# V of the strided groups read back from a DRAM scratch, and rotary partners by a DVE shuffle

## The chip, the cores and the metric
The kernel runs on one core of one Trainium2 chip. The metric is device time in microseconds (us). Three runs of the kernel before gave 2353.53, 2354.49 and 2354.59 us; the median is 2354.49.

## The reference
The reference is a chain of one gated convolution block (three branches: pooling, short convolution, long convolution) and two attention layers with a convolutional feed-forward net, for 512 tokens of width 1024, all in float32. The change lies in the attention part of the two layers. Cut to it:

```python
proj = h @ w_in[l]                     # (512 x 1024) @ (1024 x 5120)
dq, dk, dv, sq, sk, sv, gate_logits = jnp.split(proj, splits, axis=-1)
dq = apply_partial_rope(dq.reshape(dshape), cos, sin)   # 3 groups, 4 heads of 64
dk = apply_partial_rope(dk.reshape(dshape), cos, sin)
# x1, x2 = first and second 8 of a head's first 16 channels:
# [x1 * cos - x2 * sin, x2 * cos + x1 * sin, rest]
y_a = dilated_attention(dq, dk, dv) @ w_proj_a[l]       # dilations 1, 4, 16
y_b = stick_breaking_attention(sq, sk, sv) @ w_proj_b[l]
```

In group g of the dilated attention a query attends to keys whose distance is a multiple of the dilation (1, 4 or 16). With 512 tokens, groups 1 and 2 attend only inside the four classes of tokens that are equal modulo 4.

## The kernel before
**Weights.** Every weight goes through one stream. SP loads chunks of 1 MB into two buffers `raw` (`chunk_load`, L559; it waits until the last piece of the chunk before the last has been split). A chunk has two pieces. ScalarE (ACT) copies a piece to float32r (`split_hi`, L448, executed at L456), VectorE (DVE) subtracts that from the original (`split_lo`, L458, executed at L463), and both parts lie in one of four buffers `whl`, three pieces ahead of use. TensorE (PE) multiplies each product in three passes: high with high, high with low, low with high (`passes`, L1582 to L1584).

**Tiles.** For most pieces `col_tile` holds the weights stationary and streams the activations `hT` (128 x 512): 24 matmuls a piece. For V (keys `sv` and `dv`) `token_tile` (L1762) does it the other way round: 128 tokens of `hT` are stationary and 256 columns of weights stream past, 48 matmuls a piece, so that V comes out with tokens on the partitions. For group 0 of `dv` the 128 tokens are neighbours; for groups 1 and 2 they are every fourth token, `slice(tb, SEQ, 4)`, so that each of the four token tiles is one class modulo 4. Tile after tile lies in two PSUM banks; ACT copies both at once into `vd` (L877).

**The loop that matters.** In each layer the list `DIL_KEYS` (L198) has 18 pieces, n = 0 to 17: six of `dq`, six of `dk`, six of `dv` (groups 0, 1, 2, two pieces each). PE, ACT and DVE each go through this list in the same order (L1824, L865, L1442), and each has hung on it the steps of the stick-breaking heads: head h has its scores behind piece 4h, its exponents behind piece 4h + 2, and its values behind piece 4h + 4. The exponents (L1807) wait for `splo`, which DVE writes in `sb_lo` (L1432, executed at L1434) in its step 4h + 1.

**Rotary partners.** ACT copies the 128 x 512 result of a `dq` or `dk` piece twice: rounded into `qhl` (L871) and in full into `qraw` (L872). DVE subtracts the two (`rope_lo`, L1400, executed at L1402). Two more PE passes multiply a permutation matrix `swap_r` with both parts (L1833, L1834) into bank 7; they stand behind the next piece. DVE then multiplies `qraw` with the cosines (L1410), bank 7 with the signed sines (L1413), and adds the two (L1420) into `qd` or `kd`, for groups 1 and 2 sorted by class.

**After the list.** PE goes on with eight units of two heads (L1884 holds their values): the scores of unit 0, then for each unit a piece of the gates, the transposes of the probabilities (L1867), the scores of the next unit, another piece of the gates, and the values (L1884), which read `vd`. On ACT stand, in this order, the last copy of V, the split of gate piece 3, and the exponentials of unit 0 (L897); on DVE the split of that piece, then the maxima (L1460, L1461). GpSimd (POOL) computes the roots of the norms (L613) and has nothing to do in the attention.

Of the kernel before, what the change touches and what calls it, by code (L numbers as in the profile page):

```python
# [31 lines left out]
P = 128  # L32
D = 1024
SEQ = 512
KT = D // P
TB = SEQ // P
LAYERS = 2
# [9 lines left out]
MASK = -1e30  # L47
TWO_PI = 2.0 * np.pi


# [4 lines left out]
for _name, _rows in VECS:  # L55
# [6 lines left out]

CONSTS = [("ident", 128), ("negtri", 128), ("swap", 128), ("sbmul", 128), ("corr", 64), ("freq", 1),
          ("sign", 1), ("sel", 256), ("mask", 512), ("sbadd", 128)]
# [8 lines left out]
def shape_constants():  # L73

    out = np.zeros((P, NCONST), np.float32)
    i = np.arange(P)

    def put(name, value):
        value = np.asarray(value, np.float32).reshape(P, -1)
        out[:, COFF[name]:COFF[name] + value.shape[1]] = value  # L80

    put("ident", np.eye(P))
    put("negtri", -(i[:, None] >= i[None, :]).astype(np.float32))
    swap = np.zeros((P, P))
    for p in range(P):
        if p % HEAD < ROPE_DIM:
            swap[p - p % ROPE_DIM + (p % ROPE_DIM + ROPE_DIM // 2) % ROPE_DIM, p] = 1.0
    put("swap", swap)
    put("sbmul", (i[:, None] < i[None, :]).astype(np.float32))
    put("sbadd", np.where(i[:, None] < i[None, :], 0.0, MASK))  # L90
    t = np.arange(16)
    put("corr", np.tile(np.concatenate([w / np.minimum(t + 1, w) for w in POOL_WINDOWS])[None], (P, 1)))
    inv = (np.float32(ROPE_THETA) ** (-np.arange(0, ROPE_DIM, 2, dtype=np.float32) / np.float32(ROPE_DIM)))
    put("freq", np.where(i % HEAD < ROPE_DIM, inv[i % (ROPE_DIM // 2)], 0.0))
    put("sign", np.where(i % ROPE_DIM < ROPE_DIM // 2, -1.0, 1.0))

    p = np.arange(256)
    put("sel", i[:, None] == 2 * (p // P) + p % P // HEAD)
    gap = i[:, None] - i[None, :]
    own = np.where(gap >= 0, 0.0, MASK)  # L100
    put("mask", np.concatenate([np.where(gap <= 0, 0.0, MASK), own, own,
                                np.where((gap >= 0) & (gap % 4 == 0), 0.0, MASK)], 1))
    return out
# [58 lines left out]
def build(nc, t, out):  # L162
# [82 lines left out]
    table = keep("table", [P, 2, SEQ])  # L245
    arena = at[0]

    negtri_r = nc.alloc_sbuf_tensor_at("negtri_r", [P, P], R, offset=tri_at)
    swap_r = nc.alloc_sbuf_tensor_at("swap_r", [P, P], R, offset=cst_at + 4 * COFF["negtri"])
    negones_r = nc.alloc_sbuf_tensor_at("negones_r", [P, P], R, offset=vcol_at)  # L250
# [47 lines left out]
    kd = over("kd", 12 * K, [P, 3, 2, SEQ])  # L298
    vd = over("vd", 24 * K, [P, 3, TB, 256])
    sbq = over("sbq", 36 * K, [P, 2, SEQ])  # L300
# [16 lines left out]
    rot = over("rot", 84 * K, [P, 2, SEQ])  # L317
    qhl = over("qhl", 48 * K, [P, 2, 2, SEQ], R)

    ff = over("ff", 0, [P, FT, 2, SEQ], R)  # L320
# [8 lines left out]
    negtri = cst[:, COFF["negtri"]:COFF["negtri"] + P]  # L329
    swapm = cst[:, COFF["swap"]:COFF["swap"] + P]  # L330
    sbmul = cst[:, COFF["sbmul"]:COFF["sbmul"] + P]
# [17 lines left out]
    with ctx:  # L349
# [5 lines left out]
        def sem(name):  # L355
# [20 lines left out]

        sp_hi, sp_lo, q_lo = sem("sp_hi"), sem("sp_lo"), sem("q_lo")
        rot_ps, rope_done, z_ps, sb_abs, sb_l, sp_ready, e_ps, sb_attn, sbo_ps, ob_hi, ob_lo = (
            sem(n) for n in ("rot_psum", "rope_done", "z_psum", "sb_abs", "sb_log", "sp_ready", "e_psum", "sb_attn",
                             "sbo_psum", "ob_hi", "ob_lo"))  # L380
# [5 lines left out]
        fconv, silu_done, ff_hi, ff_lo = (sem(n) for n in ("ffn_conv", "silu_done", "ff_hi", "ff_lo"))  # L386
        s_out, s_frow = sem("out_done"), sem("frow_in")
        dve_chain, act_chain, pool_chain = sem("dve_chain"), sem("act_chain"), sem("pool_chain")

# [209 lines left out]
        @block.gpsimd  # L599
        def _(pool):  # L600
            load_vectors(pool, [v for v in VECS if v[0] in SECOND_VECS], s_vec2)
            nc.gpsimd.memset(neghalf, -0.5).then_inc(pool_chain, 1)
            pool.wait_ge(pool_chain, 1)

            def first_lo(tb):

                pool.wait_ge(h_hi, 8 + tb + 1)
                nc.gpsimd.tensor_tensor(hT[:, 1, :, tb * P:(tb + 1) * P], cols8(xw(2, tb)), hT[:, 0, :, tb * P:(tb + 1) * P].bitcast(F),
                                        ALU.subtract).then_inc(h_lo, 1)

            for i_, (s, tb) in enumerate(ORDER):
                pool.wait_ge(s_ms, i_ + 1)
                nc.gpsimd.tensor_tensor(rstd[:, tb:tb + 1], msq[:, tb:tb + 1], neghalf[:, 0:1], ALU.pow).then_inc(s_rstd, 1)  # L613
                if (s, tb) == (1, 3):
                    first_lo(0)
                if s == 2 and tb >= 2:
                    first_lo(tb - 1)
                if (s, tb) == (2, 3):
                    first_lo(3)


        @block.scalar
        def _(act):
# [191 lines left out]
            for l in range(LAYERS):  # L815
# [49 lines left out]
                for n_, key in enumerate(DIL_KEYS(l)):  # L865
                    split_hi(W[key] + 3)
                    if key[0] in ("dq", "dk"):
                        w_wait_full(act, key)
                        if n_ >= 2:
                            act.wait_ge(rope_done, 12 * l + n_ - 1)  # L870
                        A(qhl[:, n_ % 2, 0, :], bank(W_BANK[key]), ACT.Copy, scale=HEAD ** -0.5 if key[0] == "dq" else 1.0)  # L871
                        A(qraw[:, n_ % 2, :], bank(W_BANK[key]), ACT.Copy,  # L872
                          scale=HEAD ** -0.5 if key[0] == "dq" else 1.0).then_inc(act_read, 1)
                    elif key[3] == 1:
                        w_wait_full(act, key)
                        b = W_BANK[key]
                        A(vd[:, key[2], :, :].rearrange("p a b -> p (a b)"), psum[:, b * SEQ:(b + 2) * SEQ], ACT.Copy).then_inc(act_read, 1)  # L877
                    h, ph = n_ // 4, n_ % 4
# [96 lines left out]
        def _(dve):  # L975
# [412 lines left out]
            for l in range(LAYERS):  # L1388
                s = 2 + 2 * l
                if l == 0:  # L1390
                    link(V.tensor_copy(negtri_r[:], negtri))
                    step(V.tensor_copy(swap_r[:], swapm))
                    step(V.tensor_copy(negones_r[:], negones[:]))
# [5 lines left out]

                def rope_lo(n_):  # L1400
                    await_read(dve, DIL_KEYS(l)[n_])
                    V.tensor_tensor(qhl[:, n_ % 2, 1, :], qraw[:, n_ % 2, :], qhl[:, n_ % 2, 0, :].bitcast(F), ALU.subtract).then_inc(q_lo, 1)  # L1402

                def rope(n_):
# [3 lines left out]
                    if n_:  # L1408
                        dve.wait_ge(rope_done, 12 * l + n_)
                    V.tensor_tensor(rot[:, 0, :], qraw[:, n_ % 2, :], table[:, 0, :], ALU.mult).then_inc(dve_chain, 1)  # L1410
                    chain[0] += 1
                    dve.wait_ge(rot_ps, 12 * l + n_ + 1)
                    link(V.tensor_tensor(rot[:, 1, :], bank(7), table[:, 1, :], ALU.mult))  # L1413
                    dst = (qd if isq else kd)[:, g, j, :]
# [27 lines left out]
                for n_, key in enumerate(DIL_KEYS(l)):  # L1442
                    split_lo(W[key] + 3)
                    if 1 <= n_ <= 12:
                        rope(n_ - 1)
                    if n_ < 12:
                        rope_lo(n_)
                    h, ph = n_ // 4, n_ % 4
# [119 lines left out]
        def _(pe):  # L1568
# [191 lines left out]
            for l in range(LAYERS):  # L1760
                s = 2 + 2 * l
                def token_tile(key, strided):  # L1762

# [7 lines left out]
                    for tb in range(TB):  # L1771
                        ts = slice(tb, SEQ, 4) if strided else slice(tb * P, (tb + 1) * P)
                        o_ = bank(b + tb // 2)[:, tb % 2 * 256:tb % 2 * 256 + 256]
# [9 lines left out]

                first_tiles([("sq", l, 0), ("sq", l, 1), ("sk", l, 0), ("sk", l, 1)], s)
                token_tile(("sv", l, 0), False)
                token_tile(("sv", l, 1), False)

# [36 lines left out]
                for n_, key in enumerate(DIL_KEYS(l)):  # L1824
                    if key[0] == "dv":
                        token_tile(key, key[2] > 0)
                    else:
                        col_tile(key, h_at(0), h_at(1))
                    if 1 <= n_ <= 12:

                        pe.wait_ge(q_lo, 12 * l + n_)
                        take(7)
                        M(bank(7), swap_r[:], qhl[:, (n_ - 1) % 2, 0, :], start=True, stop=False)  # L1833
                        M(bank(7), swap_r[:], qhl[:, (n_ - 1) % 2, 1, :], start=False, stop=True).then_inc(rot_ps, 1)  # L1834
                        give(7, rope_done, 12 * l + n_)
                    h, ph = n_ // 4, n_ % 4
# [35 lines left out]
                def dil_values(u):  # L1872
                    j, b = u // 4, u % 4
                    if u == 0:
                        await_read(pe, ("dv", l, 2, 1))
                    if b == 0:
# [3 lines left out]
                    for c in range(first_, 4):  # L1880
                        for e in range(2):
                            hs = slice((2 * j + e) * HEAD, (2 * j + e + 1) * HEAD)
                            v = vd[:, 0, b - 1 + c, hs] if c < 2 else vd[:, c - 1, b, hs]
                            ins = M(bank(6 + c // 2)[e * HEAD:(e + 1) * HEAD, b * P:(b + 1) * P], v, probT[:, e, c * P:(c + 1) * P],  # L1884
# [93 lines left out]
```

## Time and profile before

| what | value |
|---|---|
| median of three runs | 2354.49 us |
| the profiled execution | 2355.59 us, span 2353.7 us |
| PE busy | 2274.0 us, 97% |
| DVE, ACT, POOL busy | 53%, 34%, 1% |
| mean granted PE clock | 0.986 |
| chain that ended last | PE 92%, DVE 5% |
| DMA | 213.8 MB, 91 GB/s over the span |

The profiled execution took 1.1 us more than the median, and its span leaves 1.9 us of it outside. "Pitch" below is the distance between the starts of two neighbouring matmuls: since they overlap in the pipeline, the duration shown for one is longer than what it adds to the time. The clock is given as a share of 2.4 GHz: 1.00 is that level and 0.50 is 1.2 GHz.

### The profile page before, as it was taken

To read this page: it belongs to the slowest core of one execution; us is meant where nothing else is said; L and a number is where in the kernel's file an instruction comes from. 1 tells how busy PE (TensorE), PEld (TensorE's weight loads), DVE (VectorE), ACT (ScalarE), POOL (GpSimd) and SP (SyncE) were. 2 spreads that over 40 slices of the span, in tenths; PEclk is the share of its full clock that TensorE was granted. 3 is DMA by queue.
4 is the path that set the end of the run, shared out by engine and by line. 5 is a ranking of instruction groups with operands and counts; after the bars stand their busy time and mean duration, and the time that the engine had idled before them with its cause. 6 is when DMAs were issued, how large, how long until landed. Compare 5 with 4: busy or idle time off the path is not lost.

```text
span 2353.7 us, 25941 instructions
## 1 busy us (share of the span) xinstructions
PE 2274.0 (97%) x10818; PEld 1875.6 (80%) x10818; DVE 1249.8 (53%) x1633; ACT 790.5 (34%) x1136; POOL 33.1 (1%) x42
## 2 busy tenths in 40 slices
PE   3999999999999799999999999999999999999998
PEld 2788888887788688987688887888798768888887
DVE  7798797923545746222745554234622274555422
ACT  1223232322532344244343333134523434333311
POOL 1000000000000300000000000000000000000000
PEclk7999999999999899999999999999999999999999
DMA  9332233332233122122123323222211212323231
GB/s 295 115 107 93 94 99 97 103 100 90 72 106 114 54 90 69 40 72 72 56 70 108 107 92 105 88 75 89 72 54 55 73 63 80 108 92 101 94 99 72
DMA packets 185554, 213.80 MB, mean 91 GB/s; under 512 B 3680, under 2 KB 165086, under 8 KB 185438
## 3 DMA queue, kind: packets, MB, share of 16 engines
q1 hardware_dynamic: 184128, 210.52, 27.3%
q8 instruction: 86, 1.41, 0.3%
q10 hardware_dynamic: 1150, 1.57, 0.2%
q14 instruction: 30, 0.25, 0.0%
q0 software_dynamic: 160, 0.06, 0.0%
HBM read 210.03 MB, written 2.10 MB: 90 GB/s over the span
## 4 chain that ended last, share of the span: by engine, by line
PE 92%; DVE 5%; issue 1%; ACT 1%; POOL 0%; DMA 0%; SPq 0%; POOLq 0%; DVEq 0%; ACTq 0%
PE psum L1582 29%; PE psum L1584 28%; PE psum L1583 28%; PE psum L1807 1%; DVE adsum L1030 1%; PE psum L1796 1%; DVE whl L463 1%; PE psum L1819 1%; PE psum L1856 1%; PE psum L1884 1%; PE psum L1867 1%; DMA x<-in_x 0%; PE psum L1912 0%; DVE stat L999 0%; POOL stat L613 0%
## 5 line engine op out<-in xcount | busy, mean ns | idle before, releaser
L1582 PE MATMUL psum<-hT,whl 128*128 128x512 f32 (+1 forms) x2112 | 803.8, 381 | 9.2 <-DVE hT L1052 6.5
L1583 PE MATMUL psum<-hT,whl 128*128 128x512 f32 (+1 forms) x2112 | 796.3, 377 | 0.0
L1584 PE MATMUL psum<-hT,whl 128*128 128x512 f32 (+1 forms) x2112 | 795.9, 377 | 0.0
L463 DVE TENSOR_TENSOR whl<-raw,whl 128x1024 fp32r<-128x1024 f32 (+1 forms) x368 | 449.4, 1223 | 642.8 <-ACT whl L456 642.8
L456 ACT ACTIVATE whl<-raw 128x1024 fp32r<-128x1024 f32 (+1 forms) x368 | 384.7, 1048 | 484.1 <-PE psum L1584 446.4
L1582 PEld LDWEIGHTS psum<-hT,whl 128*128 128x128 f32 x2112 | 398.4, 189 | 91.4 <-DVE hT L1052 9.8
L1584 PEld LDWEIGHTS psum<-hT,whl 128*128 128x128 f32 x2112 | 398.4, 189 | 73.6
L1583 PEld LDWEIGHTS psum<-hT,whl 128*128 128x128 f32 x2112 | 398.6, 189 | 71.2 <-issue 0.7
L1582 PE MATMUL psum<-whl,hT 128*128 128x256 f32 (+1 forms) x384 | 139.9, 364 | 10.0 <-DVE gates L1532 6.2
L1582 PE MATMUL psum<-whl,ff 128*128 128x512 f32 x352 | 139.9, 397 | 2.2 <-DVE fsil L1561 2.2
L1583 PE MATMUL psum<-whl,ff 128*128 128x512 f32 x352 | 139.5, 396 | 0.0
L1584 PE MATMUL psum<-whl,ff 128*128 128x512 f32 x352 | 139.5, 396 | 0.0
L1583 PE MATMUL psum<-whl,hT 128*128 128x256 f32 (+1 forms) x384 | 138.1, 360 | 0.0
L1584 PE MATMUL psum<-whl,hT 128*128 128x256 f32 (+1 forms) x384 | 137.9, 359 | 0.0
L1582 PEld LDWEIGHTS psum<-whl,hT 128*128 128x128 f32 x384 | 91.5, 238 | 17.7 <-DVE gates L1532 7.0
L1584 PEld LDWEIGHTS psum<-whl,hT 128*128 128x128 f32 x384 | 91.6, 238 | 5.4
L1583 PEld LDWEIGHTS psum<-whl,hT 128*128 128x128 f32 x384 | 91.7, 239 | 5.0
L1093 DVE SCALAR_TENSOR_TENSOR hc<-glu,vcol,hc 128x512 f32<-128x512 f32 x120 | 89.3, 744 | 0.0
L1093 DVE SCALAR_TENSOR_TENSOR acc<-glu,vcol,acc 128x512 f32<-128x512 f32 x112 | 83.3, 744 | 0.1
L1552 DVE TENSOR_SCALAR facc<-apad,vcol 128x512 f32<-128x512 f32 x44 | 24.0, 547 | 110.9 <-ACT fsil L962 53.0
L1582 PEld LDWEIGHTS psum<-whl,ff 128*128 128x128 f32 x352 | 66.3, 188 | 18.9 <-issue 3.0
L1584 PEld LDWEIGHTS psum<-whl,ff 128*128 128x128 f32 x352 | 66.3, 188 | 16.2
(269 smaller groups left out, 2198.2 us busy)
## 6 DMA issues: line engine op xcount, KB each, us to landing
raw<-in_w_in SPq DMA_DIRECT2D x88, 1024.0 KB, 5.1
raw<-in_w_up SPq DMA_DIRECT2D x44, 1024.0 KB, 5.1
raw<-in_w_down SPq DMA_DIRECT2D x20, 1024.0 KB, 5.0
ada<-in_w_ada SPq DMA_DIRECT2D x12, 1024.0 KB, 11.0
raw<-in_w_branch SPq DMA_DIRECT2D x12, 1024.0 KB, 5.1
raw<-in_w_out SPq DMA_DIRECT2D x12, 1024.0 KB, 5.0
x<-in_x SPq DMA_DIRECT2D x4, 512.0 KB, 7.4
raw<-in_w_proj_b SPq DMA_DIRECT2D x2, 1024.0 KB, 4.9
```

Of the source, the lines that this page charges most:

```text
L456: nc.scalar.activation(whl_view(w, 0), raw_view(w), ACT.Copy).then_inc(w_hi, 1)
L463: nc.vector.tensor_tensor(whl_view(w, 1), raw_view(w), whl_view(w, 0).bitcast(F), ALU.subtract).then_inc(w_lo, 1)
L1030: ins = V.scalar_tensor_tensor(o_, at_k(k), cact[:, k:k + 1], o_, ALU.mult, ALU.add)
L1093: last[dst is acc1] = step(V.scalar_tensor_tensor(A_(dst), g[:, k:k + SEQ], col("cf_w", 8 * k + tt), A_(dst), ALU.mult, ALU.add))
L1552: link(V.tensor_scalar(facc[:], apad[:, j, 2:2 + SEQ], cw(2), col("conv_b", FT * l + f), ALU.mult, ALU.add))
L1582: M(out_, stat_hi, mov_hi, start=start, stop=False, **kw)
L1583: M(out_, stat_hi, mov_lo, start=False, stop=False, **kw)
L1584: return M(out_, stat_lo, mov_hi, start=False, stop=stop, **kw)
L1796: M(bank(2 + kb)[:, 0:SEQ - kb * P], sbk[rows, h // 2, kb * P:(kb + 1) * P], sbq[rows, h // 2, kb * P:], start=True, stop=True, skip_group ...
L1807: M(bank(2 + kb)[:, (jb - kb) * P:SEQ - kb * P], (negtri_r if jb == kb else negones_r)[:], part[:, SBO[jb]:SBO[jb + 1]], start=False, stop ...
L1819: ins = M(bank(6)[po:po + HEAD, kb * P:], sbv[:, kb, h * HEAD:(h + 1) * HEAD], sba[:, SBO[kb]:SBO[kb + 1]], start=kb == 0, stop=kb == TB - ...
L1856: ins = M(bank(2 + e)[:, a:z], qd[heads, g, j, b * P:(b + 1) * P], kd[heads, g, j, k0:k0 + z - a], start=False, stop=g == 2, skip_group_ch ...
```

## The change
The pieces of `dv` for groups 1 and 2 are computed from neighbouring tokens, like group 0. ACT copies them to `vnat`, waits for its own copy, and writes them with a DMA from its queue to a DRAM scratch `v_by_token`. POOL waits for that DMA and reads the scratch back into `vc`, four neighbouring rows to a partition, so that partition u holds tokens 4u to 4u + 3 and class r is a contiguous slice. The first values of PE wait for both reads. The permutation matrix, its two matmuls, `qhl`, the second copy of ACT and `rope_lo` are gone; DVE makes the partners with a shuffle of `qraw` inside blocks of 32 partitions. The matrix leaves the constants, and the working memory behind them begins at a multiple of 128 bytes.

```diff
-    arena = at[0]
+    arena = (at[0] + 127) // 128 * 128
...
-    vd = over("vd", 24 * K, [P, 3, TB, 256])
+    vd = over("vd", 24 * K, [P, TB, 256])
+    vc = over("vc", 28 * K, [P, 2, TB, 256])
+    vnat = over("vnat", 80 * K, [P, 2, TB, 256])
+    v_dram = nc.dram_tensor("v_by_token", (LAYERS, 2, SEQ, 256), F)
...
+                if s in (2, 4) and tb == 3:
+                    l = s // 2 - 1
+                    for g in range(2):
+                        pool.wait_ge(v_out[g], 16 * (l + 1))
+                        pool.dma_start(vc[:, g, :, :], v_dram[l, g].rearrange("(u r) n -> u r n", r=TB)).then_inc(v_class, 16)
...
-                        A(qhl[:, n_ % 2, 0, :], bank(W_BANK[key]), ACT.Copy, scale=HEAD ** -0.5 if key[0] == "dq" else 1.0)
...
-                        A(vd[:, key[2], :, :].rearrange("p a b -> p (a b)"), psum[:, b * SEQ:(b + 2) * SEQ], ACT.Copy).then_inc(act_read, 1)
+                        g = key[2]
+                        if g == 1:
+                            act.wait_ge(rope_done, 12 * l + 12)
+                        dst = vnat[:, g - 1, :, :] if g else vd[:]
+                        A(dst.rearrange("p a b -> p (a b)"), psum[:, b * SEQ:(b + 2) * SEQ], ACT.Copy).then_inc(act_read, 1)
+                        if g:
+                            await_read(act, key)
+                            act.dma_start(v_dram[l, g - 1].rearrange("(b p) n -> p b n", p=P), vnat[:, g - 1, :, :]).then_inc(v_out[g - 1], 16)
...
-                    V.tensor_tensor(rot[:, 0, :], qraw[:, n_ % 2, :], table[:, 0, :], ALU.mult).then_inc(dve_chain, 1)
-                    chain[0] += 1
-                    dve.wait_ge(rot_ps, 12 * l + n_ + 1)
-                    link(V.tensor_tensor(rot[:, 1, :], bank(7), table[:, 1, :], ALU.mult))
+                    swapped = step(V.stream_shuffle(rot[:, 1, :], qraw[:, n_ % 2, :], ROPE_SWAP))
+                    step(V.tensor_tensor(rot[:, 0, :], qraw[:, n_ % 2, :], table[:, 0, :], ALU.mult))
+                    dve.wait_ge(dve_chain, swapped)
+                    link(V.tensor_tensor(rot[:, 1, :], rot[:, 1, :], table[:, 1, :], ALU.mult))
...
-                    if n_ < 12:
-                        rope_lo(n_)
...
-                        ts = slice(tb, SEQ, 4) if strided else slice(tb * P, (tb + 1) * P)
+                        ts = slice(tb * P, (tb + 1) * P)
...
-                    if 1 <= n_ <= 12:
-
-                        pe.wait_ge(q_lo, 12 * l + n_)
-                        take(7)
-                        M(bank(7), swap_r[:], qhl[:, (n_ - 1) % 2, 0, :], start=True, stop=False)
-                        M(bank(7), swap_r[:], qhl[:, (n_ - 1) % 2, 1, :], start=False, stop=True).then_inc(rot_ps, 1)
-                        give(7, rope_done, 12 * l + n_)
...
-                        await_read(pe, ("dv", l, 2, 1))
+                        await_read(pe, ("dv", l, 0, 1))
+                        pe.wait_ge(v_class, 32 * (l + 1))
...
-                            v = vd[:, 0, b - 1 + c, hs] if c < 2 else vd[:, c - 1, b, hs]
+                            v = vd[:, b - 1 + c, hs] if c < 2 else vc[:, c - 2, b, hs]
```

## Rows read from the trace of the kernel before

**Rows 1.** The page: busy times, and the chain that ended last by engine.
```profile
PE 2274.0 (97%) x10818; PEld 1875.6 (80%) x10818; DVE 1249.8 (53%) x1633; ACT 790.5 (34%) x1136; POOL 33.1 (1%) x42
...
PE 92%; DVE 5%; issue 1%; ACT 1%; POOL 0%; DMA 0%; SPq 0%; POOLq 0%; DVEq 0%; ACTq 0%
```
**Rows 2.** Windows: length, PE, PEld, DVE, ACT, POOL busy, clock, DMA, GB/s.
```profile
879.10:910.70 31.60, 31.60 (x145) 24.81 (x145) 20.42 (x31) 16.01 (x30) 0.00 (x0) 1.00 0.21 67
943.70:1003.00 59.30, 58.14 (x277) 55.54 (x278) 11.68 (x16) 15.35 (x26) 0.00 (x0) 0.97 0.11 36
```
**Rows 3.** PE's weight loads: V of neighbouring, then of strided tokens.
```profile
945.90:951.90 6.00, 5.81 (x48) 1.00 0.00 0
...
967.40:989.90 22.50, 22.42 (x97) 1.00 0.15 47
```
**Rows 4.** PE in order of time: end of n = 13, all n = 14.
```profile
951.67 0.28 PE L1584 MATMUL psum<-whl,hT 128*128 128x256 f32 x1
953.11 0.48 PE L1582 MATMUL psum<-whl,hT 128*128 128x256 f32 x1 [1.16 <-ACT vd L877]
...
964.40 0.40 PE L1807 MATMUL psum<-sphi,negtri_r 128*128 128x512 f32 x1
```
**Rows 5.** PE: the permutation's two matmuls behind n = 1.
```profile
855.29 0.40 PE L1833 MATMUL psum<-qhl,swap_r 128*128 128x512 f32 x1
855.52 0.40 PE L1834 MATMUL psum<-qhl,swap_r 128*128 128x512 f32 x1
855.76 0.40 PE L1582 MATMUL psum<-hT,whl 128*128 128x512 f32 x1
```
**Rows 6.** DVE in order of time, step n = 5 of layer 0 (head 1).
```profile
889.16 1.12 DVE L1420 TENSOR_TENSOR qd<-rot 128x512 f32<-128x512 f32 x1
890.11 0.69 DVE L1402 TENSOR_TENSOR qhl<-qraw,qhl 128x512 fp32r<-128x512 f32 x1
890.71 1.48 DVE L1434 TENSOR_TENSOR splo<-sbs,sphi 128x1280 fp32r<-128x1280 f32 x1
```
**Rows 7.** Loads of L1807 in head 1; a DVE operation with one input.
```profile
L1807 PEld LDWEIGHTS psum<-sphi,negtri_r x4: 188/202/203, 893.1 to 896.0; 128*128 128x128 f32 x4
...
L1552 DVE TENSOR_SCALAR facc<-apad,vcol 128x512 f32<-128x512 f32 x44 | 24.0, 547 | 110.9 <-ACT fsil L962 53.0
```
**Rows 8.** ACT, then PE: list's end to first values, layer 0.
```profile
1003.92 1.02 ACT L877 ACTIVATE vd<-psum 128x1024 f32<-128x1024 f32 x1 [9.88 <-PE psum L1584]
...
1009.94 0.21 ACT L897 ACTIVATION_READ_ACCUMULATOR prob<-psum,stat 128x1 f32 x1
...
1010.59 0.81 PE L1867 MATMUL psum<-cst,prob 128*128 128x128 f32 x6
...
1018.53 0.88 PE L1884 MATMUL psum<-probT,vd 128*64 128x128 f32 x12
```
**Rows 9.** DMA issues: size, median us to landing; one issue on ACT.
```profile
x<-in_x SPq DMA_DIRECT2D x4, 512.0 KB, 7.4
...
raw<-in_w_down SPq DMA_DIRECT2D x4, 512.0 KB, 3.7
out<-x SPq DMA_DIRECT2D x4, 512.0 KB, 2.6
...
7.97 0.36 ACTq L636 DMA_DIRECT2D table<-in_b_ada  x1
```
**Rows 10.** POOL: its dearest DMA issue, and its first work after attention.
```profile
1.26 0.72 POOL L532 DMA_DIRECT2D vstage<-in_norm_mix  x1 [0.82 <-POOLq L1970]
...
1190.90 0.55 POOL L613 TENSOR_TENSOR stat<-stat 128x1 f32<-128x1 f32 x1 [372.88 <-DVE stat L1281]
```
**Rows 11.** What SP's queue waited for, in the whole span.
```profile
SPq L563 <- DVE whl L463: 2195.1, 186, 31.2
```
**Rows 12.** Windows within n = 14: PE busy, clock, DMA.
```profile
955.00:957.00 2.00, 2.00 (x11) 0.50 0.00 0
957.00:959.00 2.00, 2.00 (x10) 0.71 0.42 108
```

More of the change, by code:

```diff
@@ L48 @@
 TWO_PI = 2.0 * np.pi
+ROPE_SWAP = [(i + ROPE_DIM // 2) % ROPE_DIM if i < ROPE_DIM else i for i in range(32)]
 VECS = [("b_in", 96), ("pool_scale", 8), ("sc_w", 24), ("sc_b", 8), ("cf_b", 8), ("cf_ln_g", 8),
@@ L60 @@
 AV, AG, BB, BC, BH, BG, CA, CB, CG, MG = (8 * i for i in range(10))
-CONSTS = [("ident", 128), ("negtri", 128), ("swap", 128), ("sbmul", 128), ("corr", 64), ("freq", 1),
+CONSTS = [("ident", 128), ("negtri", 128), ("sbmul", 128), ("corr", 64), ("freq", 1),
           ("sign", 1), ("sel", 256), ("mask", 512), ("sbadd", 128)]
@@ L83, in shape_constants @@
     put("negtri", -(i[:, None] >= i[None, :]).astype(np.float32))
[L84 to L88, printed above, removed]
     put("sbmul", (i[:, None] < i[None, :]).astype(np.float32))
@@ L245, in build @@
     table = keep("table", [P, 2, SEQ])
-    arena = at[0]
+    arena = (at[0] + 127) // 128 * 128
     negtri_r = nc.alloc_sbuf_tensor_at("negtri_r", [P, P], R, offset=tri_at)
-    swap_r = nc.alloc_sbuf_tensor_at("swap_r", [P, P], R, offset=cst_at + 4 * COFF["negtri"])
     negones_r = nc.alloc_sbuf_tensor_at("negones_r", [P, P], R, offset=vcol_at)
@@ L317, in build @@
     rot = over("rot", 84 * K, [P, 2, SEQ])
-    qhl = over("qhl", 48 * K, [P, 2, 2, SEQ], R)
     ff = over("ff", 0, [P, FT, 2, SEQ], R)
@@ L329, in build @@
     negtri = cst[:, COFF["negtri"]:COFF["negtri"] + P]
-    swapm = cst[:, COFF["swap"]:COFF["swap"] + P]
     sbmul = cst[:, COFF["sbmul"]:COFF["sbmul"] + P]
@@ L375, in build @@
         row_full, row_read, s_ln, s_rt, s_pos, s_tab = (sem(n) for n in ("row_full", "row_read", "lnrow_in", "rot_steps", "pos_in", "tables_ready"))
-        sp_hi, sp_lo, q_lo = sem("sp_hi"), sem("sp_lo"), sem("q_lo")
-        rot_ps, rope_done, z_ps, sb_abs, sb_l, sp_ready, e_ps, sb_attn, sbo_ps, ob_hi, ob_lo = (
-            sem(n) for n in ("rot_psum", "rope_done", "z_psum", "sb_abs", "sb_log", "sp_ready", "e_psum", "sb_attn",
+        sp_hi, sp_lo = sem("sp_hi"), sem("sp_lo")
+        rope_done, z_ps, sb_abs, sb_l, sp_ready, e_ps, sb_attn, sbo_ps, ob_hi, ob_lo = (
+            sem(n) for n in ("rope_done", "z_psum", "sb_abs", "sb_log", "sp_ready", "e_psum", "sb_attn",
                              "sbo_psum", "ob_hi", "ob_lo"))
@@ L387, in build @@
         s_out, s_frow = sem("out_done"), sem("frow_in")
+        v_out, v_class = [sem("v_by_token_out0"), sem("v_by_token_out1")], sem("v_by_class_in")
         dve_chain, act_chain, pool_chain = sem("dve_chain"), sem("act_chain"), sem("pool_chain")
@@ L1391, in _ @@
                     link(V.tensor_copy(negtri_r[:], negtri))
-                    step(V.tensor_copy(swap_r[:], swapm))
                     step(V.tensor_copy(negones_r[:], negones[:]))
@@ L1398, in _ @@
                     split_lo(W[key] + 3)
-                def rope_lo(n_):
-                    await_read(dve, DIL_KEYS(l)[n_])
-                    V.tensor_tensor(qhl[:, n_ % 2, 1, :], qraw[:, n_ % 2, :], qhl[:, n_ % 2, 0, :].bitcast(F), ALU.subtract).then_inc(q_lo, 1)
                 def rope(n_):
@@ L1761, in _, with token_tile @@
                 s = 2 + 2 * l
-                def token_tile(key, strided):
+                def token_tile(key):
                     w = W[key]
@@ L1784, in _ @@
                 first_tiles([("sq", l, 0), ("sq", l, 1), ("sk", l, 0), ("sk", l, 1)], s)
-                token_tile(("sv", l, 0), False)
-                token_tile(("sv", l, 1), False)
+                token_tile(("sv", l, 0))
+                token_tile(("sv", l, 1))
                 def sb_scores(h):
@@ L1825, in _ @@
                     if key[0] == "dv":
-                        token_tile(key, key[2] > 0)
+                        token_tile(key)
                     else:
                         col_tile(key, h_at(0), h_at(1))
-                    if 1 <= n_ <= 12:
-                        pe.wait_ge(q_lo, 12 * l + n_)
-                        take(7)
-                        M(bank(7), swap_r[:], qhl[:, (n_ - 1) % 2, 0, :], start=True, stop=False)
-                        M(bank(7), swap_r[:], qhl[:, (n_ - 1) % 2, 1, :], start=False, stop=True).then_inc(rot_ps, 1)
-                        give(7, rope_done, 12 * l + n_)
                     h, ph = n_ // 4, n_ % 4
```

## The prediction
> **What bounds the kernel.** I read the page first: PE is busy 97% of the span and holds 92% of the chain that ended last [rows 1]. What PE does not execute is saved, and what the other engines do costs nothing until PE waits for it. Then the windows over the list of 18 pieces [rows 2]: a head's four steps take 31.6 us, all of them PE, with DVE at 20.4 and ACT at 16.0. The stretch of the V pieces takes 59.3 us; there DVE and ACT are nearly idle, and PEld, the weight loads, is busy nearly as long as PE. So I looked at the loads alone. With neighbouring tokens 48 loads take 5.81 us, 0.121 us each; with every fourth token 97 take 22.42, 0.231 each [rows 3]. Matmul shape, banks and engine are the same; the step of the stationary operand is what differs. In order of time the strided piece n = 14 lasts from 953.11 to 964.40, 11.3 us [rows 4]. One more thing is in the windows: at 955 to 959 the granted clock was at 0.50 and then 0.71 [rows 12], that is, at the 1.2 GHz level for some 3.4 us, shortly after PE had waited 1.16 us [rows 4], and the strided matmuls kept their pace (11 and 10 in 2 us). They were held by their loads and not by the array.
>
> **The change part by part.**
>
> *V from neighbouring tokens.* Four pieces a layer lose the stride, eight in all. A strided piece costs 48 x 0.231 = 11.1 us by the loads [rows 3] and 11.3 us by the start times [rows 4]; I take 11.25. A piece of neighbours costs 48 x 0.121 = 5.8. That is 8 x 5.45 = **43.6 us off**, all on PE's path. ACT and DVE have to follow at 5.8 us a piece, but they do so in the heads' steps, where a quarter of 31.6 us is 7.9 us for more work than stands here (11.7 us of DVE in 59.3 [rows 2]). SP's queue waits for DVE's splits 186 times [rows 11]: weights come early, at 67 GB/s in a head and 36 here. The wait of 1.16 us for the copy of group 0's V out of banks 0 and 1 [rows 4] stays, for the banks stay.
> The Trainium skill (SBUF — State Buffer, section Door 1: The DMA port swizzle) says that SBUF has lines of 16 bytes and wants two hits in each, yet also that one may stride for free as far as "4 fp32", which is the old step. By its first half the trace agrees, 0.231 against 0.121; by its second the stride was free and nothing of the 43.6 us would come. The rows decide for the first.
>
> *The permutation matmuls.* 24 pairs, each 0.47 us from 855.29 to 855.76 [rows 5]: **11.3 us off**. The first copy of ACT, the subtraction on DVE (0.69, in effect 0.60 from 890.11 to 890.71 [rows 6]) and DVE's wait for PE go too, for nothing by themselves: both engines have room in a head [rows 2]. Weight and matrix constants at the start: 64 KB less to load, nothing.
>
> *The shuffle.* It takes the place of the subtraction in DVE's queue, and behind it, in each head's second step, stands `splo`, for which PE's exponents wait. In head 1 `splo` ends at 890.71 + 1.48 = 892.19 and PE loads for it at 893.1 [rows 6, 7]: 0.9 us of slack. PE now comes two pairs earlier, 0.93 us, so the slack is gone, and what the shuffle takes beyond 0.60 PE waits for. This counts for heads 1 and 2 of both layers, four times; head 0 has a cheaper, unstrided add, and head 3 has no rope before its `splo`. No row shows a shuffle. From below 0.547 (one input, 128 x 512 [rows 7]), from above 1.12 (the strided add [rows 6]): 0 to 0.5 us each, 0 to 2 us in all. I take it like the subtraction it replaces, 0.69, for it reads and writes the same 128 x 512: **0.4 us added**.
> The Trainium skill (VectorE: DVE Perf Modes, section The perf-mode tier table) gives a shuffle about 2400 ns for 2048 elements a partition, by estimate 0.6 us for 512, which would make this 0.0 to 0.2 us; no row here shows it.
>
> *The writes.* ACT waits for the end of its copy (which otherwise overlaps the next by 0.1 us), then issues a DMA, 0.36 us for 512 KB at the start [rows 9]. For group 1 nothing urgent is behind it. For group 2 there is: ACT's split of gate piece 3, DVE's split and maxima, ACT's exponentials, PE's transposes. That chain ends at 1009.94 + 0.21 = 1010.15, and the transposes run from 1010.59, their load some 0.2 earlier [rows 8]: 0.2 us of slack against some 0.55 of delay. **0.7 us added** over two layers (0 if the issue is hidden, 1.5 if it takes the 0.72 of POOL's dearest issue [rows 10]).
>
> *The round trip.* The first values stand 14.6 us behind the start of the last V copy (1003.92 to 1018.53 [rows 8]). In that time: the copy and its wait 1.1; the write; POOL's issue 0.72 [rows 10]; the read. For 512 KB the rows have 2.6 (a store to DRAM), 3.7 (a load alone) and 7.4 (four loads at once at the start) [rows 9]. The write at 3.7, since a weight chunk may run beside it, and the read at 3.7: 1.1 + 3.7 + 0.7 + 3.7 = 9.2 us, covered with 5 us to spare. At 7.4 twice it is 16.6, 2.0 us late a layer, 4.0 in all. So **0, at most 4 us**. The cover is two gate pieces, a score unit and the transposes; without it all 9.2 us would show in each layer. Group 1's trip begins two pieces earlier. POOL's queue: its wait stands behind the norm of the layer and before its next root at 1190.90 [rows 10], some 180 us later. The other way about, 4 MB more beside 213.8: weights may land a few us later, while SP had been waiting for DVE, not for data [rows 11].
>
> *The clock.* The slow stretch was free because the strided loads held the pace. With neighbours nothing shows that holds them but the clock, so I take their 0.121 as doubled at 1.2 GHz: 3.4 us hold 14 matmuls instead of 28, **1.7 us lost**, in layer 0 if the stretch comes again; each further one would cost the same. None may come: 0 to 5 us.
>
> **The sum.** 43.6 + 11.3 = 54.9 off; 0.4 + 0.7 + 1.7 = 2.8 back; 52.1 net. The profiled execution took 2355.6 us: 2303.5. It stood 1.1 above the median, so beside 2354.5 I forecast **2302 us**. The bound above which a measurement of this kernel can be told from no change is 0.2%, 4.7 us.
>
> **Rivals.**
> 1. *The cover fails and the small waits add up.* The round trip shows by 4 us, the shuffle is dear (2 us, 1.6 more than taken), the clock falls twice more (3.4): 2302 + 9 = 2311 us. For it: the slack before `splo` is nil by my own working, and no row shows a DRAM write followed by a read. Against it: 5 us to spare in the trip. Chance 0.12.
> 2. *The stride was not what held the pace* (or the new loads are held as before): only the permutation's 11.3 us go, less 1.1 for the waits: 2354.5 - 10.2 = 2344 us. It is also what the page's "4 fp32" would give. Against it: everything but the stride is alike in [rows 3], and the pace did not follow the clock [rows 12]. Chance 0.03.
> 3. *Slower: PE stands at the first values until V is back.* The mechanism is one chain, ACT, DRAM, POOL, DRAM, with POOL's queue as the place where it could hang. A layer gains 26 us, so the point from which it decides is a read that lands 14.6 + 26 = 41 us behind the last copy, where I expect 9. At 50 us the stall is 35.4 a layer, 71 in all: 2354.5 - 52 + 71 = 2373 us. Against it: no transfer of 512 KB took over 7.4 us [rows 9]. Chance 0.02.
>
> **How the numbers follow.** The forecast has 0.83; its own range is 2298 (none of the 2.8 us, less 1 or 2 for scatter) to 2306. The range to give reaches to rival 1, 2298 to 2311, and leaves out some 0.1. Faster by over 0.2%: the forecast and rivals 1 and 2, 0.97. Within 0.2%: 0.01, a trip of just about 41 us. Slower: 0.02.
>
> **What the profile after would show.** The stretch of V without its strides: 48 loads of `hT` in 5.8 us for every piece, the stretch down from 59.3 to about 37 us. Four steps of a head at 29.7 instead of 31.6. No L1833. PE idle before the exponents under 0.2 us in heads 1 and 2. PE idle before the first values: none; reads landed some 9 us behind the start of the last copy. The transposes of unit 0 some 0.3 us late. I am wrong if the loads stay at 0.23, if a wait of several us stands before L1884, or if DVE's shuffle takes over 1.1 us.

## The result and the profile after

The changed kernel takes **2295.49 us** (median of 4 runs, 2294.41 to 2298.57) against 2354.54 for the kernel before, run beside it (4 runs, 2353.53 to 2356.69): the ratio is 0.975, interval 0.9733 to 0.9767. The forecast was 2302 us with a range of 2298 to 2311. The direction and nearly all of the size are right, and the time lies 2.5 us below the range. The profiled execution took 2294.44 us, span 2292.6, 61.1 less than before.

The page of the kernel after: busy times.
```profile
PE 2214.4 (97%) x10758; PEld 1822.4 (79%) x10770; DVE 1250.4 (55%) x1656; ACT 779.0 (34%) x1112; POOL 35.4 (2%) x46
```
Beside [rows 1]: 48 weight loads fewer, the 24 pairs of the permutation; PE 59.6 us less busy and still at 97%. It also holds 91% of the chain that ended last. The bound is the same engine, so nearly the whole saving is time in which PE is no longer busy.

Windows after, with the columns of [rows 2]: four steps of head 1, then the stretch of the V pieces.
```profile
877.40:907.20 29.80, 29.80 (x137) 23.32 (x137) 20.50 (x34) 14.05 (x26) 0.00 (x0) 1.00 0.22 72
938.20:976.00 37.80, 36.64 (x279) 34.03 (x279) 11.69 (x16) 15.47 (x26) 0.63 (x1) 1.00 0.25 84
```
31.6 us became 29.8 and 59.3 became 37.8, as foretold (29.7 and about 37). In the head eight matmuls are gone (the four pairs); the stretch of V has as many as before, but for two at the window's edges. PE is idle there for 1.16 us, as before. The clock stands at 1.00 in both windows: the slow stretch of [rows 12] is not there.

PEld's window after, inside that stretch: pieces that were strided.
```profile
955.70:968.10 12.40, 12.35 (x105) 1.00 0.17 54
```
Loads now come every 0.12 us here too, where [rows 3] had 0.231 for the strided ones.

Where the 61.1 us of the profiled spans went, read from the starts of the same instructions:

| stretch | before | after | difference |
|---|---|---|---|
| start to the scores of head 0, layer 0 | 847.37 | 847.53 | +0.2 |
| from there to the first values, layer 0 | 171.16 | 143.92 | -27.2 |
| the same in layer 1 | 171.16 | 143.93 | -27.2 |
| all the rest (8 units, feed-forward nets) | | | -6.8 |

The 27.2 are 5.6 in the three full heads (31.65, 31.64, 32.93 to 29.77, 29.80, 31.07), 16.4 in head 3, in which three strided pieces stood (46.36 to 30.01), and 5.3 in what follows (28.58 to 23.27). The last line of the table, 6.8 us outside the attention lists, has no counterpart in the prediction.

### The profile page after: what moved, and what is told of

Read it like the earlier page. It is cut to its first block, busy times and chain, and to the rows that moved or that the text cites. A ratio compares the mean times of both kernels' runs of the same rounds, so it can differ in the third digit from the quotient of the medians.

```text
span 2292.6 us, 25818 instructions
## 1 busy us (share of the span) xinstructions
PE 2214.4 (97%) x10758; PEld 1822.4 (79%) x10770; DVE 1250.4 (55%) x1656; ACT 779.0 (34%) x1112; POOL 35.4 (2%) x46
## 4 chain that ended last, share of the span: by engine, by line
PE 91%; DVE 6%; ACT 1%; issue 1%; POOL 0%; DMA 0%; SPq 0%; ACTq 0%; POOLq 0%; DVEq 0%
PE psum L1582 28%; PE psum L1583 28%; PE psum L1584 28%; DVE whl L459 1%; PE psum L1807 1%; DVE adsum L1037 1%; PE psum L1796 1%; PE psum L1819 1%; PE psum L1878 1%; PE psum L1849 1%; PE psum L1860 1%; DMA x<-in_x 0%; DVE stat L1006 0%; PE psum L1906 0%; ACT whl L452 0%
## 5 line engine op out<-in xcount | busy, mean ns | idle before, releaser
L1582 PE MATMUL psum<-whl,hT 128*128 128x256 f32 (+1 forms) x384 | 123.7, 322 | 8.8 <-DVE gates L1532 5.0
L1584 PE MATMUL psum<-whl,hT 128*128 128x256 f32 (+1 forms) x384 | 122.3, 319 | 0.0
L1583 PE MATMUL psum<-whl,hT 128*128 128x256 f32 (+1 forms) x384 | 122.3, 318 | 0.0
L1582 PEld LDWEIGHTS psum<-whl,hT 128*128 128x128 f32 x384 | 73.1, 190 | 16.1 <-DVE gates L1532 5.8
L1582 PEld LDWEIGHTS psum<-whl,ff 128*128 128x128 f32 x352 | 66.3, 188 | 18.3 <-issue 3.0
L1584 PEld LDWEIGHTS psum<-whl,ff 128*128 128x128 f32 x352 | 66.3, 188 | 15.3
L1583 PEld LDWEIGHTS psum<-whl,ff 128*128 128x128 f32 x352 | 66.4, 189 | 15.3
L1584 PEld LDWEIGHTS psum<-whl,hT 128*128 128x128 f32 x384 | 73.1, 190 | 5.1
## 6 DMA issues: line engine op xcount, KB each, us to landing
ada<-in_w_ada SPq DMA_DIRECT2D x12, 1024.0 KB, 10.1
```

The source lines that it names most:

```text
L1582: M(out_, stat_hi, mov_hi, start=start, stop=False, **kw)
L1583: M(out_, stat_hi, mov_lo, start=False, stop=False, **kw)
L1584: return M(out_, stat_lo, mov_hi, start=False, stop=stop, **kw)
```

## The experiments

**The two halves, each alone.** The first keeps V as before, the second keeps the permutation; neither has the aligned start.
```diff
# rotary_only = before, and (the main lines)
-                    pe.wait_ge(q_lo, 12 * l + n_)
-                    M(bank(7), swap_r[:], qhl[:, (n_ - 1) % 2, 0, :], ...)
-                    M(bank(7), swap_r[:], qhl[:, (n_ - 1) % 2, 1, :], ...)
...
+                    swapped = step(V.stream_shuffle(rot[:, 1, :], qraw[:, n_ % 2, :], ROPE_SWAP))
# v_only = before, and (the main lines)
-                        ts = slice(tb, SEQ, 4) if strided else slice(tb * P, (tb + 1) * P)
+                        ts = slice(tb * P, (tb + 1) * P)
...
+                            act.dma_start(v_dram[l, g - 1]..., vnat[:, g - 1, :, :])
...
+                        pool.dma_start(vc[:, g, :, :], v_dram[l, g]...)
```


> Theory A (each part is worth the PE time it removes, and the parts add): 24 pairs of 0.467 us, 11.2 us less than the kernel before, about 2343.3 us; the stretch of a head's four steps goes from 31.6 to 29.8 us, the strided V pieces stay at 11.3 us each. Theory B (the shuffle was only free because something else in the change made room, for example the constants or the new place of the working memory): PE stands before the exponents of heads 1 and 2 and the gain is under 10 us.

> Theory A: eight pieces of 5.42 us, 43.3 us less than the kernel before, about 2311.2 us, with no wait of PE before the first values. Theory B (half of the gain outside of the list, 6.6 us in the profiled execution, hangs on the shorter V stretch, as by less granted clock lost behind it): about 50 us less, 2304.5 us.

rotary_only took 2342.59 us (ratio 0.9948, 0.9934 to 0.9961; before 2355.15 here): 12.6 off. v_only took 2311.89 (0.9812, 0.9799 to 0.9826): 43.3 off. Both terms stand at the size they were given, 11.3 and 43.6, within the scatter, and both act by themselves. The profiled execution of v_only, at 2307.69 us, is 3.8 faster than the next of its four runs; windows of it below are of that one.

**The third part of the change, alone and left out.** The diff has one more line, which moves the start of the working memory to a multiple of 128 bytes.
```diff
# align_only = before, and            (after_unaligned = after with this line undone)
-    arena = at[0]
+    arena = (at[0] + 127) // 128 * 128
```


> Theory A (the working memory's start, 32 bytes off a multiple of 64 in the kernel before and on a multiple of 128 after, sets a small part of the pace of every matmul that reads from it): the matmuls with ff as the stationary operand go from 0.2347 to 0.2329 us each, those with yahl from 0.2336 to 0.2332, together 2.5 us less, about 2352.0 us. Theory B (the place does nothing, what was gained outside of the list is scatter of the clock): paces as before and 2354.5 us within 0.5.

> Theory A: the changed kernel without the new start of its working memory loses 2.5 us, about 2298.0 us, and the matmuls with ff go back to 0.2347 us each. Theory B: as the changed kernel, 2295.5 us within 1, and the pace stays at 0.2329.

align_only: 2350.02 us over 10 runs (0.9977, 0.9968 to 0.9987), 5.1 off. after_unaligned: 2301.18 (2300.67 to 2301.59; 0.9771, 0.9757 to 0.9784), 5.7 above the change. From both sides the line is worth 5 to 6 us, and without it the kernel takes what the prediction had added up, 2302. The gain past the forecast is this line. It is more than was expected of it: 2352.0 and 2298.0 us would have been 2.5 us either way, from the pace of the matmuls alone. The next runs ask what it does.

**Is it the place from which PE reads?** In the second half of each feed-forward net PE loads `ff` (stationary), which lies in the working memory that starts at `arena`, and streams the weights `whl` past it, which lie ahead of it. By the program's addresses `whl` and `hT` leave 128 when divided by 512, and the arena 480 before and 0 after. All the tiles in question lie at multiples of 512 bytes behind these starts. The starts of the `ff` matmuls stand 0.2343 us apart before and 0.2324 after, where the clock is at 1.00. Three runs put the arena elsewhere:
```diff
-    arena = (at[0] + 127) // 128 * 128
+    arena = (at[0] + 127) // 128 * 128 + 64       # arena_64; + 128, + 256 alike
```


> The changed kernel with its working memory 64 bytes further on, so on an odd multiple of 64 instead of a multiple of 128. Theory A (a multiple of 64 is enough): the matmuls with ff stay at 0.2325 us, the time at 2295.5 within 1. Theory B (it takes 128): the pace goes to 0.2342 as it does 32 bytes off, and the time to about 2301 us.

> The changed kernel with its working memory at an address that leaves 128 modulo 512, which is also what the start of the weight buffers whl leaves. So far the pace of the matmuls with ff went 0.2342, 0.2325, 0.2292 us for starts that leave 480, 0 and 64, that is 160, 128 and 64 bytes short of whl's. Theory A (the load and the stream disturb each other unless they are in step, and the distance from whl modulo 512 sets how much): the distance is nought, the pace that of hT with whl, 0.2267, on 1056 matmuls 6.1 us less than the changed kernel, about 2289.4 us. Theory B (only the remainder by 64 counts, and 64 was better for a reason of its own): 0.2292 to 0.2325 and 2292 to 2295.5 us.

> The same with a start that leaves 256 modulo 512, 128 bytes beyond whl's. Theory A: as far off as the changed kernel on the other side, so 0.2325 us with ff and about 2295.5 us. Theory C (the further on the better, whatever whl does): 0.2267 us or less, about 2289 us.

A fourth leaves the arena at the distance from `whl` that it has in arena_128 and moves both:
```diff
-    base = (nc.sbuf_base + 63) // 64 * 64
+    base = (nc.sbuf_base + 63) // 64 * 64 + 128   # with the arena + 128: all at 256
```


> The kernel of the run before with everything 128 bytes further on: hT, whl and the working memory all leave 256 modulo 512. With whl left in place, a working memory at 256 had 0.2325 us. Theory A (what counts is the distance between the operand that is loaded and the one that streams, modulo 512): it is nought again, so 0.2267 us for hT and ff alike and 2288.8 us within 1.5. Theory D (the remainder 128 is good in itself, 256 is not): ff at 0.2325, and hT, which so far had 0.2267, too; some 7000 matmuls by 0.006, 40 us more, about 2330 us.

| kernel | arena, `whl` modulo 512 | `ff` pace, us | median us (range) |
|---|---|---|---|
| after_unaligned | 480, 128 | 0.2343 | 2301.18 (2300.67 to 2301.59) |
| after | 0, 128 | 0.2324 | 2295.49 (2294.41 to 2298.57) |
| arena_256 | 256, 128 | 0.2324 | 2297.29 (2294.34 to 2298.28) |
| arena_64 | 64, 128 | 0.2289 | 2293.91 (2293.22 to 2295.43) |
| arena_128 | 128, 128 | 0.2268 | 2288.75 (2288.71 to 2289.34) |
| all_256 | 256, 256 | 0.2268 | **2286.80** (2285.72 to 2287.84) |

The `ff` matmuls of PE in the kernel after and in arena_128 (all_256 has 390 ns too): shape, count, busy and mean ns of one, idle before.
```profile
L1582 PE MATMUL psum<-whl,ff 128*128 128x512 f32 x352 | 139.2, 396 | 2.2 <-DVE fsil L1561 2.2
```
```profile
L1582 PE MATMUL psum<-whl,ff 128*128 128x512 f32 x352 | 137.3, 390 | 2.2 <-DVE fsil L1561 2.2
```
The group of the three passes' first is 352 of the 1056 matmuls; it was 139.9 us in the kernel before. Eighty microseconds of nothing but such matmuls show it more plainly, for PE alone, first after, then arena_128:
```profile
1431.40:1511.40 80.00, 80.00 (x346) 1.00 0.27 92
```
```profile
1429.20:1509.20 80.00, 80.00 (x354) 1.00 0.27 92
```
Same clock, same DMA share, PE never idle, eight matmuls more in the same time. So the pace follows where the two operands lie. arena_256 and all_256 have the same arena remainder and two paces, which excludes a rule for the arena's own remainder. What counts in these six is the **distance** between the loaded and the streamed operand, taken here modulo 512: none 0.2268, 64 bytes 0.2289, 128 either way 0.2324, 160 0.2343. arena_64 had been expected to keep 0.2325 or to fall back to 0.2342, and did neither.

Two things more stand in the same traces. The first block has 768 matmuls of this shape with one operand at a multiple of 512 bytes in the arena; from the starts they come every 0.2267 us at no distance, but at 64 bytes every 0.2333, as at 128 (0.2332 to 0.2333). A group of them in arena_64, where arena_128 has 389 ns:
```profile
L1582 PE MATMUL psum<-yahl,whl 128*128 128x512 f32 x64 | 25.2, 394 | 0.0
```
There `whl` is loaded and `yahl` streamed, but the 192 with a loaded `mhi` and `mlo` do not gain at 64 bytes either. So a distance of nought is the fast case for all of them, while 0.2289 at 64 bytes holds for `ff` alone. And `poolhl`, streamed in 48 matmuls of the first block, lies 320 bytes beyond a multiple of 512 in the arena. In arena_64 it is thus 256 bytes from `whl`, and there its matmuls come every 0.2266 us, the fast pace; in the kernel after, 192 bytes off, every 0.2333. So 256 bytes apart is as good as none, on these 48 matmuls, and the pattern seems to repeat every 256 and not only every 512 bytes. Why distance counts (both are read from the same memory at once) is argued, not shown.

The time of arena_128 is not the pace of `ff` alone, though 1056 x (0.2324 - 0.2268) = 5.9 us comes near the 6.7 between the medians. By the starts in the two profiled executions, 5.7 us apart, the branches of the first block take 3.9 us less, what follows up to the scores of layer 0 1.3 less, and the second halves of the feed-forward nets 5.8 less together; the stretch from the first `obT` matmul of each layer to the first `ff` takes 2.3 and 2.4 us more. all_256 has the same paces and that longer stretch in one layer only. Its median of 2286.80 lies 2.0 us below the expected 2288.8, outside the 1.5 allowed.

**Is the rest in the projections?** Of the 6.8 us, the pace of `ff` explains 1.9 (0.9 and 1.0 us in the two nets). Another 2.8 and 2.1 us stand in the stretches with the projections behind the gates of the two layers, where the granted clock differs. (The pace in the first block is worth 0.7 more, but that lies ahead of the scores of layer 0, and that part as a whole is 0.2 longer.) To see whether that follows from the place of what they read, `oaT` and `obT` were moved by 32 bytes, out of line in the kernel after, into line in after_unaligned:
```diff
-    oaT = over("oaT", 80 * K, ...)
+    oaT = over("oaT", 80 * K + 32, ...)           # obT: 88 * K + 32
```


> The changed kernel, with only oaT and obT, the operands of the projections behind the gates, 32 bytes off. Theory A (half of what the place is worth comes from the projections, where slower matmuls and a longer stretch at the low clock go together): 2.5 to 3 us a layer back, about 2300 us, while the matmuls with ff stay at 0.2325. Theory B (the low clock there follows something else, and the place acts by the pace alone): 96 matmuls a layer by 0.0015 us, 0.3 us in all, 2295.8 us.

> The mirror image: the changed kernel with its working memory 32 bytes off, except for oaT and obT, which lie on a multiple of 64. Theory A: 2.5 to 3 us a layer better than the unaligned one (2301.2), about 2296 us, while the matmuls with ff stay at 0.2342. Theory B: 2300.9 us.

In the kernels these lines stand `oaT` and `obT` 96 bytes from `whl` instead of 128, and 128 instead of 160. proj_unaligned 2296.93 (2296.68 to 2299.02; 0.9751, 0.9736 to 0.9765), proj_aligned 2300.64 (2299.69 to 2301.45; 0.9763, 0.9747 to 0.978): they moved by 1.4 and 0.5 us, where 5 to 6 were expected if the place did it, so it is not what makes the difference. Windows from 8 us ahead of the first `obT` matmul to the transposes behind the projections, layer 0, PE alone: before, v_only, after, after_unaligned, and arena_128.
```profile
1010.50:1194.00 183.50, 177.87 (x920) 0.97 0.22 71
```
```profile
989.50:1170.10 180.60, 176.18 (x919) 0.98 0.23 76
```
```profile
983.50:1164.10 180.60, 175.79 (x913) 0.98 0.22 76
```
```profile
983.70:1167.10 183.40, 178.57 (x918) 0.96 0.22 75
```
```profile
978.90:1161.90 183.00, 177.04 (x912) 0.97 0.22 75
```
The same work takes 180.6 or 183 to 183.5 us, and the longer one has the lower mean clock. In the clock record of the traces, layer 0 has two stretches of 3.4 us each at the 1.2 GHz level in the short form (v_only, after), but one of 6.8 and another of 3.4 (before, arena_128) or 6.8 (after_unaligned) in the long one. v_only is unaligned and has the short form; arena_128 is aligned and has the long one in both layers. So alignment alone does not choose between them. Nor does the kernel: double_read, described below, has every operand where the kernel after has it, and in its profiled execution layer 0 took 2.3 us longer there. The four runs of the kernel after fit that, 2294.4 us at a mean clock of 0.986, 2296.5 at 0.985 and 2298.6 at 0.984, as do those of v_only, 2307.7 at 0.988 and 2311.5 to 2312.4 at 0.985 or 0.986. The difference is 2 to 3 us a layer, and **what chooses stays open**. That the aligned start brings more than its 2.5 us of pace is measured; that the rest comes by the clock is what these windows suggest, in profiled executions of one each.

**What the loads cost by their stride.** Before against after compares steps of 4 and 1. One more kernel takes the steps between, in group 1 two tokens, in group 2 three. Its V is of the wrong tokens, so it tells the time alone:
```diff
-                        ts = slice(tb * P, (tb + 1) * P)
+                        step_ = key[2] + 1 if key[0] == "dv" and key[2] else 1
+                        first_t = tb * P if step_ == 1 else tb
+                        ts = slice(first_t, first_t + step_ * (P - 1) + 1, step_)
```


> The changed kernel, but group 1 of V takes every second and group 2 every third token as stationary operand (so V is of the wrong tokens). Before, every fourth token (16 bytes apart) cost 0.231 us a matmul, neighbours 0.121. Theory A (the load pays for each 16-byte line of SBUF that it hits only once, as the Trainium skill says in SBUF - State Buffer, section Door 1): every second token has two hits in a line and stays at 0.121, every third lies between 0.121 and 0.231. Theory B (any step over 1 breaks the fast read): 0.23 for both.

One run, 2307.5 us (before 2356.02). PEld's windows: step 2, then step 3.
```profile
956.00:961.00 5.00, 5.00 (x43) 1.00 0.00 2
...
973.00:981.00 8.00, 8.00 (x46) 1.00 0.00 0
```
From the starts, a load at step 2 comes every 0.120 us, at step 3 every 0.1754, at step 4 every 0.231 to 0.2335, neighbours every 0.120. A load takes 128 words a partition; they touch 32, 64, 96 and 128 lines of 16 bytes. 0.1754 / 96 and 0.2335 / 128 both give 1.82 ns a line, and steps 1 and 2 lie at 0.120, the pace of the 256-column matmul. So the stride can be counted by the lines it touches, hidden up to two words' step. The expectation had counted the lines that are hit only once (none, none, 64 and 128): 0.120 plus 0.88 ns for each gives 0.1763 and fits the same four points, and no run tells the two counts apart. The Trainium skill (SBUF — State Buffer, section Door 1: The DMA port swizzle) has the lines of 16 bytes and the two hits; step 2 makes just two hits, and was free here.

**How near the round trip is to the end of its cover.** POOL waits for both reads, then reads group 2 (index 1 of the scratch) once more, and PE waits for that third read too:
```diff
+                    pool.wait_ge(v_class, 48 * l + 32)
+                    pool.dma_start(vc[:, 1, :, :], v_dram[l, 1]...).then_inc(v_class, 16)
...
-                        pe.wait_ge(v_class, 32 * (l + 1))
+                        pe.wait_ge(v_class, 48 * (l + 1))
```


> The changed kernel, but POOL waits for both reads of the scratch and then reads group 2 once more, and PE's first values wait for the third read too. In the changed kernel the second read lands 10.1 us behind the start of the last V copy and the first values stand 14.9 us behind it: 4.8 us to spare. Theory A (the trip is covered because it is short enough, and a third read of 6.0 to 6.4 us is too much by 1.3 to 1.7): PE stands that long before the first values in each layer, 2.6 to 3.4 us in all and as much again if the clock falls, 2298 to 2302 us. Theory B (the cover is larger than it looks, for example because the third read finds the DMA rings free and lands in under 4.8): no wait, 2295.5 us.

2297.0 us (2295.48 to 2298.49; 0.9751, 0.9735 to 0.9767): not to be told from the change. In double_read, POOL at the third read and PE at the first values, and then the landing of all reads of `vc`, from the view of that tile:
```profile
985.83 0.53 POOL L622 DMA_DIRECT2D vc<-v_by_token  x1 [5.72 <-DMA vc<-v_by_token]
990.36 0.44 PE L1880 MATMUL psum<-probT,vd 128*64 128x128 f32 x4
```
```profile
DMA to landing us min/median/max: 3.4/6.0/6.5
```
The third read, with no weight chunk beside it, takes 3.4 us and is in at 989.2, 1.1 us ahead of its first reader. The change's own trip can thus be 3 us or more longer at no cost.

## Why the prediction was right, and where it was wrong

**V: right.** 43.6 us foretold, 43.3 in v_only, 21.7 in each layer of the profile. The rival that the stride was not what held the pace falls with it and with the steps 2 and 3.

**Permutation: right.** 11.3 foretold, 5.6 a layer and 12.6 in rotary_only, which includes scatter.

**Shuffle: size about right, its effect smaller.** DVE after in order of time, the step that answers to [rows 6], and PE's loads behind it as in [rows 7]:
```profile
886.13 0.76 DVE L1412 STREAM_SHUFFLE rot<-qraw 128x512 f32<-128x512 f32 x1
886.76 0.68 DVE L1413 TENSOR_TENSOR rot<-qraw,table 128x512 f32<-128x512 f32 x1
...
889.02 1.49 DVE L1436 TENSOR_TENSOR splo<-sbs,sphi 128x1280 fp32r<-128x1280 f32 x1
```
```profile
L1807 PEld LDWEIGHTS psum<-sphi,negtri_r x4: 186/203/205, 890.6 to 893.4; 128*128 128x128 f32 x4
```
The shuffle takes 0.76 us, the next operation starts 0.63 behind it; I had taken 0.69. `splo` ends at 890.51 and PE loads at 890.6 without waiting. The slack is all but gone, as foretold, yet the 0.4 us did not come. The Trainium skill (VectorE: DVE Perf Modes, section The perf-mode tier table) gave by estimate 0.6, which the trace bears out by the distance of the starts.

**The writes: nearly right.** Scores of unit 0 to the transposes: 6.87 us before, 7.12 after, 0.5 for both layers against 0.7.

**The round trip: the result right, its parts not.** ACT, SP, POOL and PE after, in order of time; below them, in a fence of their own, the page's rows of the two transfers, count, size and median us to landing.
```profile
976.54 1.02 ACT L881 ACTIVATE vnat<-psum 128x1024 f32<-128x1024 f32 x1 [4.27 <-PE psum L1584]
977.59 0.38 ACTq L884 DMA_DIRECT2D v_by_token<-vnat  x1
...
980.42 0.37 SPq L559 DMA_DIRECT2D raw<-in_w_in  x1
980.66 0.53 POOL L620 DMA_DIRECT2D vc<-v_by_token  x1 [13.34 <-DMA v_by_token<-vnat]
...
991.45 0.44 PE L1878 MATMUL psum<-probT,vd 128*64 128x128 f32 x4
```
```profile
v_by_token<-vnat ACTq DMA_DIRECT2D x4, 512.0 KB, 2.8
vc<-v_by_token POOLq DMA_DIRECT2D x4, 512.0 KB, 6.4
```
The write took 2.8 where I had 3.7, the read 6.0 here (median 6.4) where I had 3.7: a weight chunk of SP started 0.24 us before it. V is back at 986.7, 10.1 us behind the start of the copy instead of 9.2, and 4.8 us before the first values. Rival 1, a failing cover, and rival 3, a read that lands 41 us or more behind the copy, were far off.

**The clock: wrong by 1.7, to the good.** I had taken the slow stretch of [rows 12] to come again and to cost 1.7; it did not come. With it gone the two lists of the profile are 27.2 us shorter each, the late transposes included: 54.4 off, against 52.1 in the sum, and after_unaligned shows 54.0 (2355.15 - 2301.18).

**The step that failed.** It is in the change part by part, as one that is not there: the line that starts the working memory at a multiple of 128 bytes got no term and no bound, though it stood in the diff. It is worth 5.1 us alone and 5.7 on top of the rest; some 2.5 of that are the pace of matmuls, and the cause of the other half stays open. From the 2301.2 of after_unaligned it leads to the measured 2295.5. The range reached from nothing of the small costs upward and had no room below for an unpriced part. The trace before held what could have priced it: at the same shape and a clock of 1.00 the matmuls that stream `hT` past `whl` start every 0.2271 us and those with `ff` every 0.2343, though it did not say that the place was the reason. The prediction's own way, to bound from both sides what no row shows, was not applied: a pace of 1056 matmuls that could change by 1 or 2% is 2 to 5 us.

**A better version.** all_256 is the change with the weights and the working memory at one remainder modulo 512 (ratio 0.9712, 0.9696 to 0.9728): 2286.80 us, 69.0 below the kernel before (2355.84, run beside it) and 8.7 below the change (2295.49, run at another time), with no run of the one among those of the other.

## What to carry to other kernels

Price every line of a diff, a change of address too: where PE is busy 97% of the time, 1% of the pace of the 1056 `ff` matmuls is 2.5 us, as much as all the small waits that were reckoned here (2.8). Look at the weight loads when matmuls are slower than their columns, and let the stationary operand lie so that a load touches few lines; a round trip through DRAM of 10 us cost nothing here, where the next reader is 15 us away. And try a few starts of the working memory against that of the weights: it is a change of one number, and brought 8.7 us.

## What the runs showed that was not expected

- The pace of the `ff` matmuls with 512 float32r columns ran from 0.2268 to 0.2343 us, 3%, by the distance between the operand that is loaded and the one that is streamed, at a clock of 1.00. Those of the first block were as fast at no distance, but gained nothing at 64 bytes over 128, and 256 bytes apart were as fast as none (0.2266).
- A stationary operand at step 2 loads as fast as at step 1 (0.120 us), at step 3 in 0.1754, at step 4 in 0.231 to 0.2335.
- The same read of 512 KB took 3.4 and 3.5 us as the third one in double_read and 6.0 to 6.9 us in the kernel after, where each time SP had started a weight chunk 0.24 us before.
- The clock falls to its lower level in one of two patterns in the projections, 180.6 or some 183 us for the same work, and in executions of kernels with the same placement; no experiment here tells what picks one.
